# Which PSUM banks the first products after a normalization use, in a two-block model kernel on one Trainium2 core

## The reference, cut to what matters

```python
h = rms_norm(x, g_pre_mix) * (1 + scale1) + shift1
...                                              # projections, convolution, retention
x = x + gate1 * rms_norm(mix, g_post_mix)        # end of stage "out"
h = rms_norm(x, g_pre_mlp) * (1 + scale2) + shift2
f = square(relu(h @ w_fc1)) @ w_fc2
x = x + gate2 * rms_norm(f, g_post_mlp)          # end of stage "fc2"
h = rms_norm(x, norm_g[0])
v, gate = split(h @ w_in)
m = grouped(multiscale_pool(v), w_grp) * scale
x = x + (m * silu(gate)) @ w_out                 # end of stage "pout"
h = rms_norm(x, norm_g[1])
q, fz, i, gate = split(h @ w_in)                 # recurrent scan in chunks over 16 heads
...
x = x + (o * silu(gate)) @ w_out                 # end of stage "hout"
out = rms_norm(x, final_g)
```

## Time and profile before

| | before |
|---|---|
| median of three runs | 1499.78 us (1496.35 to 1500.8) |
| profiled execution | 1499.84 us, span 1498.1 us |
| granted TensorE clock, mean | 0.992 |
| PE busy | 1450.9 us, 97% |
| DVE busy | 870.7 us, 58% |
| ACT busy | 564.0 us, 38% |
| chain that ended last | PE 92%, DVE 4%, ACT 1%, DMA 1%, issue 1% |

### The profile page before, as it was taken

The page is one execution under the profiler, slowest core; times in us unless marked ns, Lnnn a source line. Parts: engine busy times, 40 slices in busy tenths (PEclk is TensorE's granted clock), DMA queues, the critical chain, the costliest instruction groups (busy, mean ns, idle before and its releaser), DMA issues.

```text
span 1498.1 us, 18490 instructions
## 1 busy us (share of the span) xinstructions
PE 1450.9 (97%) x7204; PEld 1207.1 (81%) x7204; DVE 870.7 (58%) x1718; ACT 564.0 (38%) x1025; POOL 0.2 (0%) x4
## 2 busy tenths in 40 slices
PE   4999998999999999899999999999999999999998
PEld 3788887988888888788888887888888888888786
DVE  7777766443333335556467434425778777788545
ACT  6423345422232224443332324333444434444332
POOL 0000000000000000000000000000000000000000
PEclk9999999999999999899999999999999999999999
DMA  8645441353223334023223333232222221222221
GB/s 328 226 154 213 178 162 55 109 201 98 88 97 99 99 98 127 29 98 97 94 91 102 102 94 100 95 98 72 70 71 71 71 69 61 70 71 71 70 70 57
DMA packets 43863, 158.31 MB, mean 106 GB/s; under 512 B 4864, under 2 KB 5248, under 8 KB 43776
## 3 DMA queue, kind: packets, MB, share of 16 engines
q1 hardware_dynamic: 43776, 157.12, 31.7%
HBM read 155.00 MB, written 2.10 MB: 105 GB/s over the span
## 4 chain that ended last, share of the span: by engine, by line
PE 92%; DVE 4%; ACT 1%; DMA 1%; issue 1%; SPq 0%; ACTq 0%; DVEq 0%
PE PS L476 28%; PE PS L478 28%; PE PS L477 28%; PE PS L760 1%; PE PS L808 1%; PE PS L771 1%; PE PS L472 1%; PE PS L812 1%; PE PS L802 1%; PE PS L780 1%; PE PS L788 1%; DVE RAW L925 1%; PE PS L827 1%; DVE WL L955 1%; DMA X<-in_x 1%
## 5 line engine op out<-in xcount | busy, mean ns | idle before, releaser
L476 PE MATMUL PS<-HH,WH 128*128 128x512 f32 (+1 forms) x1088 | 432.3, 397 | 0.0
L478 PE MATMUL PS<-HH,WL 128*128 128x512 f32 (+1 forms) x1088 | 418.3, 384 | 0.0
L477 PE MATMUL PS<-HL,WH 128*128 128x512 f32 (+1 forms) x1088 | 417.2, 383 | 0.0
L955 DVE TENSOR_TENSOR WL<-RAW,WH 128x1024 fp32r<-128x1024 f32 x219 | 266.1, 1219 | 73.6 <-ACT WH L1659 73.3
L1659 ACT ACTIVATE WH<-RAW 128x1024 fp32r<-128x1024 f32 x219 | 230.7, 1057 | 184.6 <-PE PS L478 145.6
L478 PEld LDWEIGHTS PS<-HH,WL 128*128 128x128 f32 x1088 | 204.5, 188 | 41.8
L476 PEld LDWEIGHTS PS<-HH,WH 128*128 128x128 f32 x1088 | 204.8, 188 | 37.7 <-issue 1.0
L477 PEld LDWEIGHTS PS<-HL,WH 128*128 128x128 f32 x1088 | 205.0, 188 | 37.1 <-issue 1.0
L476 PE MATMUL PS<-WH,ZH 128*128 128x512 f32 x400 | 155.9, 390 | 0.0
L478 PE MATMUL PS<-WH,ZL 128*128 128x512 f32 x400 | 155.6, 389 | 0.0
L477 PE MATMUL PS<-WL,ZH 128*128 128x512 f32 x400 | 155.6, 389 | 0.0
(11 more groups left out here) (259 smaller groups left out, 1788.1 us busy)
## 6 DMA issues: line engine op xcount, KB each, us to landing
RAW<-in_w_fc SPq DMA_DIRECT2D x64, 512.0 KB, 3.5
RAW<-in_hgrn_in SPq DMA_DIRECT2D x64, 512.0 KB, 3.5
RAW<-in_ada SPq DMA_DIRECT2D x43, 512.0 KB, 4.5
RAW<-in_pool_in SPq DMA_DIRECT2D x40, 512.0 KB, 3.6
RAW<-in_w_in SPq DMA_DIRECT2D x27, 512.0 KB, 4.1
RAW<-in_pool_out SPq DMA_DIRECT2D x16, 512.0 KB, 3.6
RAW<-in_hgrn_out SPq DMA_DIRECT2D x16, 512.0 KB, 3.5
RAW<-in_w_out SPq DMA_DIRECT2D x8, 512.0 KB, 4.1
```

The source lines that it names most:

```text
L476: e.matmul(out, wh, xh, start=first, stop=False)
L477: e.matmul(out, wh, xl, start=False, stop=False)
L478: return e.matmul(out, wl, xh, start=False, stop=last)
L955: e.tensor_tensor(lo, raw(i), hi.bitcast(F32), ALU.subtract).then_inc(taken.sem, taken(i))
```

## The change

Bank numbers are changed, and two calls change places. Both pairs of transposes go to banks 0 to 3. The first projection after each border writes to banks 4 to 7 (at "pout": 4 and 5, then 6 and 7), and all later banks follow by four small functions. In ScalarE's `boundary` the squares of token tile 2 stand ahead of the square of bank (3, 1) instead of behind it.

```diff
+        def hidden_bank(f):
+            return 4 + f if f < 4 else (f - 4) % 7
+
+        def pool_bank(g, j):
+            return j if g else 4 + j
+
+        def gate_bank(g, j):
+            return 4 + j if g else j
+
+        def value_bank(g, j):
+            return j if g % 2 else 4 + j
...
# TensorE, transposed
-                for i in range(4):
-                    b = 4 * q + i
+                for b in range(4):
                     claim(b)
-                    for f in (i, i + 4):
+                    for f in (b, b + 4):
...
-                    m.then_inc(banks.full[b], banks.fill((stage, "t", q, i), b))
+                    m.then_inc(banks.full[b], banks.fill((stage, "t", q, b), b))
...
# TensorE, the stages
-            run(halved([("fc1", j) for j in range(4)], [0, 1, 2, 3], False, "out"))
+            run(halved([("fc1", j) for j in range(4)], [hidden_bank(j) for j in range(4)], False, "out"))
...
-                run(column(("fc1", f), f % 7))
+                run(column(("fc1", f), hidden_bank(f)))
...
-                    run(halved([("pv", 0, j) for j in range(4)], [0, 1, 2, 3], False, "fc2"))
+                    run(halved([("pv", 0, j) for j in range(4)], [pool_bank(0, j) for j in range(4)], False, "fc2"))
...
-                        run(column(("pv", g, j), j))
+                        run(column(("pv", g, j), pool_bank(g, j)))
...
-                    run(column(("pg", g, j), 4 + j))
+                    run(column(("pg", g, j), gate_bank(g, j)))
...
-                        claim(f)
+                        b, cols = pool_bank(g, f), slice(128 * i, 128 * i + 128)
+                        claim(b)
...
-                to = [0, 1, 2, 3] if g % 2 == 0 else [4, 5, 6, 7]
+                to = [value_bank(g, j) for j in range(4)]
...
# VectorE, lows (and ScalarE, highs, in the same way)
-                            out=HL[:, f, c], in0=PS[4 * q + i][:, 256 * (f // 4):256 * (f // 4) + 256],
+                            out=HL[:, f, c], in0=PS[i][:, 256 * (f // 4):256 * (f // 4) + 256],
...
-                        m.then_inc(banks.free[4 * q + i], 1)
+                        m.then_inc(banks.free[i], 1)
...
# ScalarE, boundary
                 out_square(3, 0)
                 hi_to(s + 3)
+                x_squares(2)
                 out_square(3, 1)
-                x_squares(2)
                 highs(stage, 0, (4, 5), gain, shift)
```

More of the change, by code:

```diff
@@ L726, in tensor_program @@
                         f = 2 * q + i
-                        cols = slice(128 * i, 128 * i + 128)
-                        claim(f)
+                        b, cols = pool_bank(g, f), slice(128 * i, 128 * i + 128)
+                        claim(b)
                         for k in range(4):
@@ L731, in tensor_program @@
                                 e.wait_ge(plow.sem, plow.of(g, k))
-                            m = three(PS[f][:, :], wh[:, k, cols], wl[:, k, cols], phi(k), plo(k),
+                            m = three(PS[b][:, :], wh[:, k, cols], wl[:, k, cols], phi(k), plo(k),
                                       k == 0, k == 3)
-                        m.then_inc(banks.full[f], banks.fill(("pm", g, f), f))
+                        m.then_inc(banks.full[b], banks.fill(("pm", g, f), b))
                     wfree[s] = banks.made(("pm", g, 2 * q + 1))
@@ L1358, in last @@
                     e.wait_ge(gate.sem, gate.of("pg", g, j))
-                    e.tensor_tensor(Z[:, 16 + j, :], Z[:, 16 + j, :], PS[4 + j][:, :], ALU.mult).then_inc(
-                        banks.free[4 + j], 1)
+                    b = gate_bank(g, j)
+                    e.tensor_tensor(Z[:, 16 + j, :], Z[:, 16 + j, :], PS[b][:, :], ALU.mult).then_inc(banks.free[b], 1)
                 late.append(last)
@@ L1407, in vector_program @@
                     for f in (2 * q, 2 * q + 1):
-                        zt = 4 * g + f
+                        zt, b = 4 * g + f, pool_bank(g, f)
                         e.wait_ge(*banks.taken(("pg", g, f)))
                         e.wait_ge(*banks.made(("pm", g, f)))
-                        e.scalar_tensor_tensor(out=Z[:, zt, :], in0=PS[f][:, :],
+                        e.scalar_tensor_tensor(out=Z[:, zt, :], in0=PS[b][:, :],
                                                scalar=VEC[:, V_PS + zt:V_PS + zt + 1], in1=Z[:, 16 + f, :],
-                                               op0=ALU.mult, op1=ALU.mult).then_inc(banks.free[f], 1)
+                                               op0=ALU.mult, op1=ALU.mult).then_inc(banks.free[b], 1)
             rows(16)
@@ L1760, in whole @@
                         e.wait_ge(hlo.sem, hlo.of(stage, (8 * q + f - 4) // 8, (f - 4) % 8))
-                    m = e.activation(T32[:, i, :], PS[4 * q + i][:, 256 * (f // 4):256 * (f // 4) + 256],
+                    m = e.activation(T32[:, i, :], PS[i][:, 256 * (f // 4):256 * (f // 4) + 256],
                                      ACT.Identity, scale=gain[:, f:f + 1], bias=shift[:, f:f + 1])
@@ L1784, in highs @@
                             e.wait_ge(hlo.sem, hlo.of(stage, q, f - 4))
-                        e.activation(HH[:, f, c], PS[4 * q + i][:, 256 * (f // 4):256 * (f // 4) + 256],
+                        e.activation(HH[:, f, c], PS[i][:, 256 * (f // 4):256 * (f // 4) + 256],
                                      ACT.Copy, scale=gain[:, f:f + 1]).then_inc(hhi.sem, hhi(stage, q, f))
@@ L1951, in relu @@
                 e.wait_ge(*banks.made(("fc1", f)))
-                e.activation(TMP[:, f % 2, :], PS[f if f < 4 else f % 7][:, :], ACT.Relu).then_inc(
-                    banks.free[f if f < 4 else f % 7], 1)
+                b = hidden_bank(f)
+                e.activation(TMP[:, f % 2, :], PS[b][:, :], ACT.Relu).then_inc(banks.free[b], 1)
             def hidden(k):
@@ L1979, in pool_values @@
                 e.wait_ge(*banks.made(("pv", g, j)))
-                e.activation(VP[:, 16:PADW], PS[j][:, :], ACT.Copy).then_inc(banks.free[j], 1)
+                b = pool_bank(g, j)
+                e.activation(VP[:, 16:PADW], PS[b][:, :], ACT.Copy).then_inc(banks.free[b], 1)
                 if j:
@@ L1987, in pool_gate @@
                     e.wait_ge(*banks.taken(("pm", g - 1, j)))
-                e.activation(Z[:, 16 + j, :], PS[4 + j][:, :], ACT.Sigmoid).then_inc(gate.sem, gate("pg", g, j))
+                e.activation(Z[:, 16 + j, :], PS[gate_bank(g, j)][:, :], ACT.Sigmoid).then_inc(gate.sem, gate("pg", g, j))
             def pooled(k):
@@ L2016, in scan_values @@
             def scan_values(g, j):
-                b = j if g % 2 == 0 else 4 + j
+                b = value_bank(g, j)
                 e.wait_ge(*banks.made(("hv", g, j)))
```

## The result

| | before | after |
|---|---|---|
| median | 1500.29 us (1496.35 to 1501.91, 4 runs) | 1481.37 us (1480.82 to 1482.02, 4 runs) |
| profiled execution | 1499.84, span 1498.1 | 1482.02, span 1480.2 |
| mean granted clock | 0.992 | 0.998 |

The ratio is 0.9878, with a 95% interval from 0.9858 to 0.9898: 18.9 us less, where 18.5 were forecast. Lines 476 to 478 of before are 488 to 490 after, L472 is L484, L1063 is L1075, L1086 is L1098, L1749 is L1761, L1761 is L1773.

The account below looks back on a forecast made before the run. TensorE, busy 97% of the span, was taken as the bound, losing time at three stage borders. Gains of 6.5 (out), 10.6 (fc2) and 1.4 (pout) sum to 18.5 us: 1499.8 - 18.5 = 1481.3 us, range 1477 to 1485.

Parts of the forecast that it names:

- Why it stood still: At the borders the first products' data is ready, but their banks are held by the first pair's transposes until read.
- Part 1: First products to banks 4 to 7: gain 6.5 us at out, 10.6 fc2, 1.4 pout, with 0.7 stall at bank 7.
- Part 2: Later steps and second pair's transposes at out and fc2: no wait; slack before the transposes 0.6 and 1.0 us.
- Part 3: Second pair's transposes to banks 0 to 3: adds no wait, 0.
- Part 4: Squares of tile 2 moved ahead on ScalarE: 0, bounds 0 and +0.4; with old banks alone some 1.1 us at out.
- Part 5 and 6: Other banks in fc1, pool stage and value groups: 0, bound 0.7 us; queues: no DMA changed, border gains should stay.
- The first rival: Clock still falls at out and fc2, by short pause or turn to 256 columns: 5.4 us more, 1486.7 us; chance 0.08.
- The slower rival: Clock stays low through the whole first group behind out and fc2: 46 us more, 1527 us; chance 0.03.

Follow-up runs that it names:

- banks_only: The changed kernel with the squares of tile 2 put back behind the square of (3, 1), so only the banks differ from before: 1481.66 us, ratio 0.9872.
- column3_late: The changed kernel with the products of bank 7 put last in the first two steps: 1479.81 us, ratio to before 0.986.
- tile3_late: The changed kernel with two more squares of tile 2 ahead of those of tile 3 at out and fc2: 1482.21 us (one run).
- squares_only: The kernel before, old banks, with only the squares of tile 2 moved ahead: 1500.88 us, ratio 0.9996.
- pout_pause: The kernel before with four more squares of tile 2 ahead of the reads of tiles 4 and 5, at pout alone: 1504.03 us (one run).
- squares_ahead_2more: The changed kernel with two more squares of tile 2 ahead of the square of (3, 1) at out and fc2: 1486.93 us (one run).
- after_again: The changed kernel run once more without an edit: 1481.24 us, ratio 0.9869.
- squares_ahead_4more: The changed kernel with four more squares of tile 2 ahead of the square of (3, 1) at out and fc2: 1492.42 us (one run).

## Why the prediction was right, point by point

**Why it stood still: right.** Banks, not data, held the first products. With only the banks changed they start right behind the last output product, and the time falls by all of the 18.6 us (banks_only).

**Part 1: right.** Forecast 6.5, 10.6 and 1.4; measured 6.44, 10.58 and 1.55. The stall at bank 7 was put at 0.7: by starts the gap is 253.18 - 252.46 = 0.72 where 0.12 is usual, so 0.60. It came out shorter because TensorE started 0.06 us behind VectorE's end (the take runs from 252.43 for 0.69), where 0.17 had been added. The product behind it starts after 0.22 instead of 0.12, which the prediction left out, and the two misses cancel: column3_late won back 0.7.

**Part 2: right.** No wait at steps 4 to 6 or at the second transposes. Their slack was put at 0.6 and 1.0 with the old order on ScalarE; it was 0.6 at out in banks_only, 1.0 and 1.1 at out and fc2 with the squares moved, and tile3_late shows that what exceeds it is paid.

**Part 3: right.** No new wait came with the second pair in banks 0 to 3.

**Part 4: right for this change, wrong beside it.** The moved squares end at 250.47, 1.2 us ahead of the square that they might have delayed, and bring nothing. These are ScalarE's rows at out of the changed kernel:

```profile
249.34 1.04 ACT L1757 ACTIVATE TMP<-X 128x1024 f32<-128x1024 f32 x1
250.28 0.19 ACT L1757 ACTIVATION_READ_ACCUMULATOR TMP<-X 128x1 f32 x1
251.71 0.60 ACT L1809 ACTIVATE TMP<-PS 128x512 f32<-128x512 f32 x1 [1.24 <-PE PS L490]
```

The aside that they alone would have given 1.1 us with the old banks failed: I followed the first wait only, though the prediction itself names bank 3 as the second one (squares_only).

**Part 5 and 6: right.** The stretches between the borders are equal to 0.03 us; no wait ahead of head 0. That nothing is lost there is shown. That bank 0 had 1.3 us to spare isn't: no run moved that claim.

**The sum was right, the match to 0.1 us was not earned.** 18.5 were forecast for the traces, the borders gave 18.57, but the spans differ by 17.9: the start took 2.28 more and the tail 1.6 less. The start: its first transposes waited 17.9 instead of 16.8 us, since a load of X on the chain that ended last took 8.85 us instead of 7.75, and the windows show a grant of 0.65 from 46 to 50 where before had 1.00. The stretch from the wait at 46 us to the wait at 163 us was 1.65 us longer for it. The tail: see the last section. The runs of the changed kernel differ by up to 3 us and those of before by up to 6, so an agreement of medians within that is luck.

**The first rival was judged on too little.** I held against it that pout's pause of 1.27 us left the clock alone (it did so again in squares_only). It is not a matter of the turn to 256 columns (pout_pause, and 1.00 after every 0.43 of the new banks), so that half of it is refuted. But a single row where a short pause did no harm doesn't show that it can't: a pause of 1.77 did harm once and once not (squares_ahead_2more). The Trainium skill (TensorE: Matmul & The Clock Gate, "A second HAM failure mode: psum-queue depth-cycling") speaks of short pauses between groups that come often. The traces show the lower level in some executions behind single pauses of 1.43 and 1.77 us, and never behind one of 0.43; no run here has them often.

Two details of this rival were off. It says that the grant fell in fc2 before the products. In the trace it fell at 617.71, 0.15 us behind the start of the first product, and only in squares_only and pout_pause did it fall while TensorE stood still there. And 5.4 us for the clock was too low: its own terms, 7.1 less five times 0.3, give 5.6, and the busy time at the lower level gives the 6.6 estimated above, which leaves little for the restarts.

**The slower rival** did not come: the grant rose again within each border, and no stretch at the lower level was longer than the 10.2 us of fc2.

## What to carry to other kernels

When the first products behind a transposition wait, ask whether for data or for a bank: if the transposed tiles still sit in the banks that the products are to fill, exchange the sets, and put last the product whose bank is freed last. Follow every bank that one step claims, not only the first, before you price an edit on the reader's engine; the wait moves to the next bank. And price a standstill of TensorE with the clock, but after pauses of 1.4 to 1.8 us treat the clock's part as one that comes or stays away from run to run.

## What the runs showed of the hardware

**The same pause is followed by the lower clock in some executions and not in others.** At head 15 TensorE waits 1.43 us in all ten traces, in identical work. The lower level follows in six (before, after_again, column3_late, squares_ahead_2more, squares_ahead_4more, pout_pause) and not in four (after, banks_only, squares_only, tile3_late). The windows right behind it in before, in after and in after_again:

```profile
1403.00:1405.00 2.00, 2.00 (x6) 1.61 (x6) 1.19 (x4) 0.00 (x0) 0.00 (x0) 0.50 0.54 111
```

```profile
1387.00:1389.00 2.00, 2.00 (x11) 1.60 (x10) 1.02 (x4) 0.00 (x0) 0.00 (x0) 1.00 0.69 197
```

```profile
1386.00:1388.00 2.00, 2.00 (x7) 1.54 (x6) 0.78 (x4) 0.00 (x0) 0.00 (x0) 0.53 0.78 252
```

after and after_again are one kernel. From the product behind this pause to the end of the span it is 96.1 to 96.2 us in the six traces with the fall and 94.5 to 94.6 in the four without, so this is where the tail's 1.6 us of the first comparison came from. It is a part of the spread between runs of one kernel: the four runs of after_again took 1479.72, 1480.55, 1481.94 and 1482.82 us with mean grants of 0.999, 0.998, 0.997 and 0.995. What decides it stays open; no run varied the moment of the pause by itself. The length alone doesn't: a wait of 1.7 us at about 163 us, also in all ten traces, was never followed by the lower level.

**At the three borders every standstill of 2.6 us and more went with a fall to the lower level** (out and fc2 of before, squares_only and pout_pause, squares_ahead_4more at both, pout_pause at pout). This is no rule for the whole span. Near 46 us TensorE waits for VectorE's lows in every trace, for 1.84 to 3.51 us, and the lower level went with it in five traces of ten. In before it didn't, though the wait was 3.02 us:

```profile
46.08 0.47 PE L476 MATMUL PS<-WH,HH 128*128 128x512 f32 x1 [3.02 <-DVE HL L1143]
```

```profile
46.00:50.00 4.00, 3.92 (x17) 3.30 (x18) 2.27 (x4) 3.66 (x5) 0.00 (x0) 1.00 1.02 412
```

In after 2.52 us at this place were followed by the fall, in after_again 1.84. Behind the first 16.8 us the record of before shows 1.00 too, though the first transposes there took 346 ns in the mean and those at the borders 273; whether the record or something else is at fault there stays open.

**What a fall costs is about half of TensorE's busy time at the lower level.** In the experiments one fall cost 1.5 to 2.2 us, 0.1 to 0.4 less than half of that busy time. fc2 of before lost more. Its border took 29.96 us, and 28.75 in squares_only with nearly the same waits. The lower level lasted equally long in both, but in squares_only it began during the standstill:

```profile
615.12:625.37 10.25, 5.66 (x23) 5.10 (x24) 6.75 (x21) 3.07 (x6) 0.00 (x0) 0.50 0.16 54
```

TensorE was busy for 5.66 us of it against 8.08 in before. Half of the difference is 1.21 us, and so is the difference of the borders. So 1.2 us of fc2's gain hung on the moment of the fall.
